# Weight slots of one kernel set 32 bytes apart from each other in SBUF

## The reference

```python
def reference(x, ...):
    x = first_block(x, ...)    # 16 meta tokens in front: 272 tokens
    return second_block(x, ...)

# first_block
proj = rmsnorm(h, norm1_g) @ w_in            # u, q, k, v and two gates
mixed = (sigmoid(g_ssm) * (s5_mixer(u) @ w_ssm_out)
         + sigmoid(g_att) * (y_att @ w_att_out))
h = h + mixed @ w_o
h = h + conv_glu_ffn(rmsnorm(h, norm2_g), w_up, conv_w, conv_b, w_down)   # inner width 2816

# second_block
z = rms_norm(x, norm_mix) @ w_in             # LRU, HGRN2 and attention groups
x = x + concat(...) @ w_out
u = square(relu(rms_norm(x, norm_mlp) @ w_ff1))      # inner width 4096
x = x + u @ w_ff2
return rms_norm(x, norm_final)
```

## Time and profile before

| | us |
|---|---|
| median of 3 runs | 740.59 |
| lowest and highest of them | 739.98, 741.73 |
| profiled execution, its time | 744.92 |
| profiled execution, its span | 743.1 |

### The profile page before, as it was taken

One profiled execution on the slowest core, in us unless ns is written; L12 is line 12 of the kernel. 1 busy time (PEld: TensorE's weight loads), 2 busy tenths in 40 slices (PEclk: granted clock), 3 DMA queues, 4 the chain that ended last, 5 costly groups with the idle time before them and its releaser, 6 DMA issues.

```text
span 743.1 us, 14560 instructions
## 1 busy us (share of the span) xinstructions
PE 709.0 (95%) x6152; PEld 665.5 (90%) x6152; DVE 537.3 (72%) x954; ACT 379.9 (51%) x564; POOL 23.9 (3%) x50
## 2 busy tenths in 40 slices
PE   6999997999989899999999999999889999999996
PEld 4988996888989899999999999888888989989995
DVE  5898669657878767777777799966867656556553
ACT  6577456448356343444443684478554344343441
POOL 3010000000000000000000150000000000000000
PEclk9999999999999999999999999999999999999999
DMA  7751243115445455555555554424245556556541
GB/s 239 213 161 59 67 162 115 59 59 158 144 153 174 154 184 172 189 204 174 174 197 197 177 171 131 153 80 132 84 162 167 201 173 208 186 187 210 174 167 56
DMA packets 94700, 115.66 MB, mean 156 GB/s; under 512 B 7971, under 2 KB 83932, under 8 KB 94636
## 3 DMA queue, kind: packets, MB, share of 16 engines
q1 hardware_dynamic: 94244, 114.51, 47.2%
q0 software_dynamic: 128, 0.13, 0.1%
q10 hardware_dynamic: 264, 0.10, 0.1%
HBM read 113.69 MB, written 1.05 MB: 154 GB/s over the span
## 4 chain that ended last, share of the span: by engine, by line
PE 78%; DVE 11%; ACT 6%; issue 3%; DMA 1%; SPq 0%; DVEq 0%; ACTq 0%
PE psum L1761 17%; PE psum L1762 16%; PE psum L1763 16%; PE psum L2299 4%; PE psum L2298 4%; PE psum L2297 4%; DVE w_lo L1060 3%; PE psum L2069 3%; PE psum L2067 3%; PE psum L2065 3%; ACT w_hi L492 2%; PE psum L1873 1%; PE psum L1908 1%; DMA xtok<-in_x_dram 1%; PE psum L2122 1%
## 5 line engine op out<-in xcount | busy, mean ns | idle before, releaser
L1060 DVE TENSOR_TENSOR w_lo<-w_raw,w_hi 128x2048 fp32r<-128x2048 f32 x105 | 240.0, 2288 | 101.0 <-ACT w_hi L492 100.7
L492 ACT ACTIVATE w_hi<-w_raw 128x2048 fp32r<-128x2048 f32 x105 | 199.8, 1907 | 58.4 <-PE psum L2299 34.5
L1761 PE MATMUL psum<-x2n_hi,w_hi 128*128 128x256 f32 x400 | 113.3, 283 | 2.1 <-DVE w_lo L1060 1.2
L1762 PE MATMUL psum<-x2n_lo,w_hi 128*128 128x256 f32 x400 | 110.9, 277 | 0.0
L1763 PE MATMUL psum<-x2n_hi,w_lo 128*128 128x256 f32 x400 | 110.8, 277 | 0.0
L1761 PE MATMUL psum<-hs_hi,w_hi 128*128 128x256 f32 (+1 forms) x352 | 100.3, 285 | 3.1 <-DVE ff L979 3.1
L1762 PE MATMUL psum<-hs_lo,w_hi 128*128 128x256 f32 (+1 forms) x352 | 99.9, 284 | 0.0
L1763 PE MATMUL psum<-hs_hi,w_lo 128*128 128x256 f32 (+1 forms) x352 | 99.8, 283 | 0.0
L1761 PEld LDWEIGHTS psum<-x2n_hi,w_hi 128*128 128x128 f32 x400 | 75.1, 188 | 5.1 <-DVE w_lo L1060 1.4
L1762 PEld LDWEIGHTS psum<-x2n_lo,w_hi 128*128 128x128 f32 x400 | 75.2, 188 | 0.7
L1763 PEld LDWEIGHTS psum<-x2n_hi,w_lo 128*128 128x128 f32 x400 | 75.3, 188 | 0.0
(11 more groups left out here) (438 smaller groups left out, 1516.9 us busy)
## 6 DMA issues: line engine op xcount, KB each, us to landing
w_raw<-in_w_ff_dram SPq DMA_DIRECT2D x32, 1024.0 KB, 5.3
w_raw<-in_w_in_dram SPq DMA_DIRECT2D x27, 1024.0 KB, 5.3
w_raw<-in_w_up_dram SPq DMA_DIRECT2D x22, 1024.0 KB, 5.1
w_raw<-in_w_down_dram SPq DMA_DIRECT2D x11, 1024.0 KB, 5.0
w_raw<-in_w_o_dram SPq DMA_DIRECT2D x4, 1024.0 KB, 5.1
w_raw<-in_w_out_dram SPq DMA_DIRECT2D x4, 1024.0 KB, 5.2
w_raw<-in_w_ssm_out_dram SPq DMA_DIRECT2D x2, 1024.0 KB, 5.2
w_raw<-in_w_att_out_dram SPq DMA_DIRECT2D x2, 1024.0 KB, 5.1
```

The source lines that it names most:

```text
L492: A.activation(w_hi[:, u % NW, :], raw[:, u % NRAW, :], ACT.Copy).then_inc(sem("hi_ready"), 1)
L1060: V.tensor_tensor(w_lo[:, u % NRAW, :], raw[:, u % NRAW, :], w_hi[:, u % NW, :].bitcast(F32), ALU.subtract).then_inc(sem("lo_ready"), 1)
L1761: T.matmul(out_, lh, rh, start=start, stop=False)
L1762: T.matmul(out_, lh, rl, start=False, stop=False)
```

## The change

Slots of `raw`, `w_lo` and `w_hi` get a length of 2056 elements instead of 2048 (`GAP` = 8 elements, 32 bytes), of which the first 2048 are used. Behind each of the two buffers the gap of the last slot is taken back (`top[0] -= 4 * GAP`). So the slots of `raw` and `w_lo` have phases 128, 160, 192 and 224, and those of `w_hi` 224, 0 and 32. The seven small buffers behind (`CT`, `ident`, `ones`, `sel`, `selT`, `p_a`, `p_b`) move up by 160 bytes, and from `C1` on every buffer has its old address, since the space of 192 bytes ahead of it is cut to 32. Instructions, their order and their number on every engine stay as they were, and so do all shapes.

```diff
@@ -55,6 +55,7 @@
 UNIT = 2048
+GAP = 8
@@ -162,9 +163,11 @@
-        raw = sb("w_raw", [P, NRAW, UNIT])
-        w_lo = sb("w_lo", [P, NRAW, UNIT], F32R, base)
-        w_hi = sb("w_hi", [P, NW, UNIT], F32R)
+        raw = sb("w_raw", [P, NRAW, UNIT + GAP])
+        w_lo = sb("w_lo", [P, NRAW, UNIT + GAP], F32R, base)
+        top[0] -= 4 * GAP
+        w_hi = sb("w_hi", [P, NW, UNIT + GAP], F32R)
+        top[0] -= 4 * GAP
@@ -172,7 +175,7 @@
-        top[0] += 192
+        top[0] += 32
@@ -367,7 +370,7 @@
-                dst = raw[:, n % NRAW, :].rearrange("p (k n) -> p k n", k=u["kk"])
+                dst = raw[:, n % NRAW, 0:UNIT].rearrange("p (k n) -> p k n", k=u["kk"])
@@ -489,7 +492,7 @@
-                    A.activation(w_hi[:, u % NW, :], raw[:, u % NRAW, :], ACT.Copy).then_inc(sem("hi_ready"), 1)
+                    A.activation(w_hi[:, u % NW, 0:UNIT], raw[:, u % NRAW, 0:UNIT], ACT.Copy).then_inc(sem("hi_ready"), 1)
@@ -1057,7 +1060,7 @@
-                    V.tensor_tensor(w_lo[:, u % NRAW, :], raw[:, u % NRAW, :], w_hi[:, u % NW, :].bitcast(F32),
+                    V.tensor_tensor(w_lo[:, u % NRAW, 0:UNIT], raw[:, u % NRAW, 0:UNIT], w_hi[:, u % NW, 0:UNIT].bitcast(F32),
@@ -1773,8 +1776,8 @@
-                wh = w_hi[:, un % NW, :].rearrange("p (k n) -> p k n", k=kk)
-                wl = w_lo[:, un % NRAW, :].rearrange("p (k n) -> p k n", k=kk)
+                wh = w_hi[:, un % NW, 0:UNIT].rearrange("p (k n) -> p k n", k=kk)
+                wl = w_lo[:, un % NRAW, 0:UNIT].rearrange("p (k n) -> p k n", k=kk)
```

More of the change, by code:

```diff
@@ L2056, in down @@
                 pe.wait_ge(sem("ff_lo"), 2 * i + 2)
-                wh = w_hi[:, un % NW, :].rearrange("p (k n) -> p k n", k=2)
-                wl = w_lo[:, un % NRAW, :].rearrange("p (k n) -> p k n", k=2)
+                wh = w_hi[:, un % NW, 0:UNIT].rearrange("p (k n) -> p k n", k=2)
+                wl = w_lo[:, un % NRAW, 0:UNIT].rearrange("p (k n) -> p k n", k=2)
                 for m in range(8):
@@ L2255, in out_first @@
                 pe.wait_ge(sem("lo_ready"), un + 1)
-                wh = w_hi[:, un % NW, :].rearrange("p (k n) -> p k n", k=8)
-                wl = w_lo[:, un % NRAW, :].rearrange("p (k n) -> p k n", k=8)
+                wh = w_hi[:, un % NW, 0:UNIT].rearrange("p (k n) -> p k n", k=8)
+                wl = w_lo[:, un % NRAW, 0:UNIT].rearrange("p (k n) -> p k n", k=8)
                 for m in range(2):
```

## The result

| | us |
|---|---|
| before, median of 4 runs beside it | 741.16 (739.98 to 742.5) |
| changed, median of 4 runs | 748.89 (748.25 to 749.08) |
| changed, profiled execution | 749.08, span 747.3 |
| ratio | 1.0101, 95% interval 1.0073 to 1.0129 |

The change costs 7.7 us, 1.0%. The forecast was 4.3 us more, and the range ended at 748.5. The sign was right, the size was not.

What follows compares the result with a forecast made beforehand. TensorE was taken to bound the kernel. 744.92 us profiled plus 4.3 from lost short spacing, other terms 0, gave 749.2; less the profile's 4.3 above the median, 744.9 us, range 732.5 to 748.5.

Steps and rivals of the forecast that it cites:

- What bounds the kernel: Whole kernel: TensorE, busy for 709.0 of 743.1 us; in both feed-forward parts extra time per matmul lengthens the kernel.
- the bound for the cover: ScalarE and VectorE in the feed-forward parts: without idle cover, 0.2 us by 53 units would be 11 us; value taken 0.
- The 4%: Weight loads: 1 KB pieces at phases off 256 bytes cost 4% more on average by the skill's rule; value taken 0.
- three quarters of 5.7: TensorE: 22 short units lose 4.2 us, 15 ff2 units 1.5; three quarters of the total is 4.3 us.
- The quarter that I left off: TensorE: pairings with high and low tile equal or 32 bytes apart, three of 12, were taken to lose nothing.
- The units that are long now stay so: 0: TensorE: units already at the long spacing (118 ns per matmul), such as up_b and `down`, neither gain nor lose.
- the difference of 4.3 us: Whole kernel: the profiled execution, 744.92 us, is 4.3 us above the median; this offset was subtracted from 749.2.
- a jump between high and low tile breaks the short spacing: TensorE: high and low tiles 64 bytes or more apart lose the 113 ns spacing for 118 ns; 4.3 us more.
- The spread of the short spacing to other units: TensorE: up_b, `down` and others reach the 113 ns spacing as high tiles move off; 734.9 or 728.4 us, chance 0.39.
- No effect: TensorE: addresses don't matter, spacings depend on when a run of matmuls begins; 740.6 us, chance 0.17.
- The third rival: TensorE: all slots go to the 12.5 ns excess of mixed phases; 748.1 us; range 746 to 750 has chance 0.15.

Runs made afterwards that it cites:

- e7: Kernel before with all weight slots at phase 0, streams unmoved, so the loaded tile lies 192 bytes from the stream; 747.42 us, ratio 1.0064.
- e1: Kernel before, unchanged, measured against itself; 743.15 us at the median of 12 executions, ratio 1.0022.
- e5: Kernel before with the whole layout moved up by 32 bytes, all distances between buffers kept; 740.52 us, ratio 0.9997.
- e3: Kernel before with all high weight slots at phase 160, low ones still at 128; 751.44 us, ratio 1.0138.
- e9: Kernel before with only x2n_hi and x2n_lo moved, from phase 64 to 32, weights still at 128; 745.13 us, ratio 1.0046.
- e12: Kernel before with u_hi and u_lo, the tiles ff2 loads, moved by 128 bytes to phase 192; 743.53 us, ratio 1.002.
- e2: Kernel before with all seven weight slots at phase 160, streams still at 64, so distance 96; 749.17 us, ratio 1.0108.
- e10: Kernel before with low and raw slots spread over phases 128, 160, 192, 224, high ones all at 128; 747.82 us, ratio 1.0081.
- e11: Kernel before with high slots spread over phases 128, 160, 192, low and raw ones all at 128; 749.48 us, ratio 1.0101.

## Why the prediction was right about the sign and wrong about the size

**What bounds the kernel: right.** The other engines and the loads stayed as they were (ScalarE's copy from a median of 1902 ns to 1906), and the units that got longer are units of TensorE. The prediction's 53 units in the bound for the cover are a slip: ff1 and ff2 are 32 units, and both feed-forward parts 65; nothing hangs on it. For the rule of the Trainium skill ("DMA: Bandwidth & Descriptors", section "How a descriptor splits into AXI transactions"), from which I worked out 4%: 47.4% of 747.3 us is 1.0% more packet time than 47.2% of 743.1. No load of ff1 and ff2 lands later at the median (5.3 us both times). With every slot at phase 0 (e7) it was 47.1% of 746.5 us, no less than in e1, 47.3% of 741.6. The 4% weren't seen; only the side that is written was moved in any of these runs.

**Where the time went.** Starts of the first matmul of up_a and of the first one behind the last `down`, in e5, which has before's distances, and in the changed kernel (us, recorded us):

```profile
232.19 0.28 PE L1761 MATMUL psum<-hs_hi,w_hi 128*128 128x258 f32 x1
```
```profile
422.09 0.28 PE L1761 MATMUL psum<-x2n_hi,w_hi 128*128 128x256 f32 x1
```
```profile
233.14 0.29 PE L1764 MATMUL psum<-hs_hi,w_hi 128*128 128x258 f32 x1
```
```profile
425.95 0.28 PE L1764 MATMUL psum<-x2n_hi,w_hi 128*128 128x256 f32 x1
```

With the start of ff1 as a third mark the four profiles divide like this (us):

| stretch | e5 | e1 | profile of before | changed |
|---|---|---|---|---|
| to the first up_a | 232.2 | 232.2 | 233.8 | 233.1 |
| first feed-forward part | 189.9 | 190.0 | 192.9 | 192.8 |
| middle | 129.7 | 129.6 | 129.5 | 130.4 |
| from the first ff1 to the end | 186.7 | 189.8 | 186.9 | 191.0 |

**The middle and the part from ff1 on: about right, by errors that cancel.** I took 4.3 us for them, three quarters of 5.7. Against the profile of before they grew by 0.9 and 4.0 us, 4.9 together. In the terms of the sum: an ff1 unit lost 0.22 us instead of 0.19 (113.9 to 118.5 ns), an ff2 0.06 instead of 0.10 (229.1 to 231.5 ns), and the middle 0.9 us where eight units by 0.19 are 1.5. The quarter that I left off, for pairings 0 or 32 bytes apart, was a mistake: none of the 14 units of ff1 kept the short spacing. 32 bytes lose it (e3), and the equal pairing at 224 has distance 160.

**The step that failed: "The units that are long now stay so: 0".** I read up_b and `down` off one execution, in which they were long, and put the sum on the median with the difference of 4.3 us between them carried along as a constant. It isn't one. Of the five profiled executions with distance 64 in up_b and `down` (before, e1, e5, e9, e12) three have these units short. The one of the lower group, where the median of before lay, is among them. There the change takes that away too: e5 needs 189.9 us for the first feed-forward part and the changed kernel 192.8, as long as the prediction's own profile. These 2.9 us are the greatest part of what was missing. Another 1.6 us of the difference that I carried along lie ahead of the first up_a (233.8 against 232.2), where the changed kernel needs 0.9 us more than e5; no run looked into that. From e5 to the changed kernel it is 0.9, 2.9, 0.7 and 4.3, which make 8.8 us, beside 7.7 between the medians. The number that should have warned me stood in my own text: a profiled execution 4.3 us above a median whose three runs lie within 1.8 us. That the lower group owes its time to short units in both parts is shown by one profile of it and argued for the rest.

The spacings alone would give more than 2.9 us: 528 matmuls of `down` by 5.2 ns and 528 of up_b by 3.2, less 0.9 ns for those of up_a, are 3.9. Part of it is hidden by the clock: from 245 to 262 us the granted clock was 0.80 in e5 and 0.90 in the changed kernel, so that e5 ran 3.4 us longer at the half clock. By my estimate, from 213 ns a matmul there and 120 at the full clock, that costs it 1.5 us. These estimates leave 0.5 us between them.

**The mechanism: the place was right, the reason wrong.** I said that a jump between high and low tile breaks the short spacing. e2 has no jump and loses it; e5 and e9 show that it is the distance between loaded tile and stream; e10 and e11 show within one execution that a unit of up_b or `down` comes down to 5.44 us only where all three loads of a product have the distance 64 (in the changed kernel some pairings reach 5.55, 115.6 ns). A jump matters only because two different tiles can't both lie 64 bytes ahead of one stream. That the sign came out right was luck in part: the jump and the distance both said slower.

**The rivals.** The spread of the short spacing to other units (0.39) didn't happen, for the reason that was given against it: other distances weren't short. No effect (0.17) is refuted by e2 against e5: the same phase of the weights, the same instructions, and ratios of 1.0108 and 0.9997. With it falls what I had drawn from the Trainium skill ("TensorE: Matmul & The Clock Gate", section "Step-by-step: what each phase is for"), that loading the next tile takes nothing from the running matmul: here the spacing depends on where the two lie to each other. The third rival, everything at the mixed excess, came nearest, 748.1, though not by its sum: of the units that were long, `down` rose by 0.7 ns, from 117.8 to 118.5, and up_b not at all, where it had 1.2; the units that are short in the lower group did the rest.

**Open.** What picks the spacing in an execution of before wasn't found. Why 64 and not 96, 128 or 192 wasn't found either. A collision for a shared store would fit that equal phases are bad for 256 columns and that the excess vanishes at half the clock. It explains neither why the farther distances are no better nor why equal phases are the best for the 512 columns of ff2. `u_hi` and `u_lo` at 128, the phase of the weights, which would give ff2 the distance 0, weren't tried.

## What to carry to other kernels

Where TensorE is busy throughout, compare the distance between the starts of matmuls of one shape over the whole program: if it varies by 4% with nothing waiting, addresses of the loaded tile and of the stream are worth a look, and their difference is what to hold fixed when a layout is changed. Padding slots apart from each other shifts that difference for each slot in turn and can only keep a good one in some of them. Which difference is the good one has to be measured for each shape: here it was 64 bytes with 256 columns and 0 with 512. And before a sum is made on one profile, look whether that execution is a typical one; if its time lies outside the spread of the others, its units may run at another spacing than in those that set the median.

## What the runs showed of the hardware

fp32r matmuls of 256 columns, each with its own 128x128 load, run at 113.3 or at 117.8 ns with the same addresses. Mostly they stay at one of the two for tens of microseconds, over a turn of other units in between; in e12 ff1 went to and fro from unit to unit. The distance between loaded tile and stream, modulo 256 bytes, decides whether the shorter one is had as a rule: for `down` 113.3 ns at 64, 118.7 at 96, 118.8 at 128, 117.8 at 192 and 120.0 at 0, though at 192 two units with x2n reached 113.3. The same distance gave the same spacing whichever of the two had been moved: 119.8 ns at 160 for `cv` and `hg_i` in e2 and e9, 233.3 and 233.1 at 64 for ff2 in e7 and e12. Moving both together by 32 bytes changes nothing (ratio 0.9997). With 512 columns streaming the order is another: 227.8 ns at 0, 229.1 at 192, 233.3 at 64. VectorE's subtraction took a median of 2291 ns with its operands at one phase and at mixed ones; ScalarE's copy went from a median of 1902 ns to 1906.
